# Dense attention with the scores turned over: keys on the partitions, 512 queries moving

## The reference

```
sc = jnp.einsum('bqkgc,bskc->bkgqs', qblk, k).astype(jnp.float32) * scale
p = jax.nn.softmax(sc, axis=-1)
return jnp.einsum('bkgqs,bskc->bqkgc', p.astype(v.dtype), v)
```

## Time and profile before

| | us |
|---|---|
| median of 3 runs (lowest, highest) | 3892.43 (3886.58, 3893.5) |
| span of the profiled execution, first to last instruction | 3884.4 |
| PE busy in the span | 3578.4 (92%) |
| DVE, ACT, POOL busy | 2522.3 (65%), 1854.0 (48%), 255.5 (7%) |
| first instruction of the dense heads to their last product | 2960.4 to 3364.9 |

### The profile page before, as it was taken

How to read it: one execution, slowest core, us unless ns; L and a number is a source line. 1 busy time by engine, 2 the same in 40 slices (tenths; PEclk the granted TensorE clock), 3 DMA queues, 4 the chain that set the end, 5 groups by cost and what they waited for, 6 DMA issues and landing times. The chain is left out here.

```text
span 3884.4 us, 57831 instructions
## 1 busy us (share of the span) xinstructions
PE 3578.4 (92%) x23078; PEld 2954.4 (76%) x23078; DVE 2522.3 (65%) x3931; ACT 1854.0 (48%) x2531; POOL 255.5 (7%) x178
## 2 busy tenths in 40 slices
PE   7999999999999999999999995999888999976996
PEld 5778888777777888877997784777787877765774
DVE  4477673498767667666325645778665766547776
ACT  4224432287334444443215742677436766533775
POOL 0000000000000000000000000233000000002342
PEclk9999999999999999999999997999899999998998
DMA  5011225532513337752413232899623130135998
GB/s 208 28 50 60 87 71 189 187 121 85 182 60 139 149 141 287 261 207 89 145 45 131 62 141 104 329 365 368 200 52 117 37 131 29 48 133 207 366 366 283
DMA packets 229433, 607.63 MB, mean 156 GB/s; under 512 B 30456, under 2 KB 130600, under 8 KB 211136
## 3 DMA queue, kind: packets, MB, share of 16 engines
q1 hardware_dynamic: 212896, 546.91, 38.4%
q0 software_dynamic: 13168, 55.16, 5.0%
q10 hardware_dynamic: 3120, 2.10, 0.2%
HBM read 483.38 MB, written 120.73 MB: 156 GB/s over the span
## 5 line engine op out<-in xcount | busy, mean ns | idle before, releaser
L4459 DVE TENSOR_TENSOR ring_r<-ring,oN_r 128x4096 fp32r<-128x4096 f32 x48 | 212.5, 4427 | 64.5 <-ACT oN_r L4365 64.5
L4459 DVE TENSOR_TENSOR ring_r<-ring,hT_r 128x4096 fp32r<-128x4096 f32 x48 | 212.3, 4424 | 62.1 <-ACT hT_r L4365 62.1
L4365 ACT ACTIVATE hT_r<-ring 128x4096 fp32r<-128x4096 f32 x48 | 174.0, 3630 | 73.1 <-DMA ring<-in_w_all 72.9
L4365 ACT ACTIVATE oN_r<-ring 128x4096 fp32r<-128x4096 f32 x48 | 174.1, 3630 | 68.0 <-DMA ring<-in_w_all 67.2
L171 PE MATMUL scans_G<-ring_r 128*128 128x512 f32 x512 | 204.6, 400 | 0.0
L1433 DVE CUSTOM_DVE_ANT_0 oN<-heads_scores,heads_table 128x1024 f32<-128x1024 f32 x128 | 156.1, 1220 | 42.5 <-issue 42.5
L173 PE MATMUL scans_G<-ring_r 128*128 128x512 f32 x448 | 175.1, 391 | 0.0
L172 PE MATMUL scans_G<-hT_r,ring_r 128*128 128x512 f32 x448 | 175.0, 391 | 0.0
L4237 POOL TENSOR_TENSOR moe_taker<-moe_zero 128x1 f32<-128x1 f32 x64 | 136.5, 2133 | 433.7 <-ACT moe_y L4444 394.0
L1388 ACT ACTIVATE oN<-oN,heads_nm 128x1024 f32<-128x1024 f32 x128 | 146.7, 1146 | 23.4 <-DVE heads_nm L1433 20.2
L172 PE MATMUL mlp_ps<-mlp_room_r,ring_r 128*128 128x512 f32 x384 | 150.4, 392 | 0.0
(11 more groups left out here) (805 smaller groups left out, 10523.0 us busy)
## 6 DMA issues: line engine op xcount, KB each, us to landing
ring<-in_w_all SPq DMA_DIRECT2D x110, 2048.0 KB, 19.1
hidden_operands<-mlp_room SPq DMA_DIRECT2D x56, 512.0 KB, 2.6
ring<-in_w_mlp SPq DMA_DIRECT2D x38, 512.0 KB, 5.5
ring<-in_w_mlp SPq DMA_DIRECT2D x8, 2048.0 KB, 8.1
ring<-in_w_all SPq DMA_DIRECT2D x12, 1024.0 KB, 6.4
branch_gates<-scans_stg SPq DMA_DIRECT2D x48, 256.0 KB, 2.0
merge_raw<-branch_gates SPq DMA_DIRECT2D x16, 768.0 KB, 5.1
ring<-hidden_operands SPq DMA_DIRECT2D x22, 512.0 KB, 3.5
```

The lines of the kernel that those rows point to most:

```text
L4365: act.activation(w_high[n % RING], buf[:, (first + n) % RING, :], ACT.Copy).then_inc(w_cast, 1)
L4459: dve.tensor_tensor(buf_r[:, b, :], buf[:, b, :], w_high[n % RING].bitcast(F32), ALU.subtract)\
```

## The change

The scores are computed with the keys on the partitions: a step takes 128 keys and 512 queries of one pair. Eight steps are a *group* (all keys for 512 queries of a pair), 16 groups in all, 128 steps (`T`). The probabilities then come out of the exponential as the product with the values needs them, so the 1024 transposes, their copies and `shift` go. What the row maximum and the row sum gave must come in other ways:

- **Maxima ahead.** `top(s)` takes the old form (128 queries, 512 keys) in one fp32r pass, for the latent heads with a second pair of products of 32 rows for the rotary part. DVE's `reduce` takes the maxima of it. These run nine steps (`LEAD`) ahead of the scores. At the end of a group PE transposes the maxima (`turn_tops`), and DVE's `shifts` spreads them with a mask.
- **Shift as rows times ones.** For grouped heads a product of 32 rows (`ones_r` with `shift_r`) puts the shift into the scores' bank before the three passes. For latent heads it rides along with the rotary part: its three passes and the shift lie on 128 partitions and are one product of 128 rows per head.
- **Sums.** GpSimd adds up the probabilities of the first seven steps of a group, six additions of 128x1024; PE's `sums` multiplies that and the eighth by ones. DVE takes the reciprocal of 128x512 and multiplies the output, which ACT has copied from PSUM (`keep`), by it.

The splits of queries and keys are cut into pieces of 512 columns (`split_low`) or 1024 (`cast`). The rotary operands use two slots of the weight ring, so during this stage only the two slots of the output projection are loaded; the first two slots of the experts' weights follow in the next stage.

```diff
-        N = PAIRS * NT
-        sc = lent[:, 0:3 * S].rearrange("p (b s) -> p b s", b=3)
-        pT = lent[:, 3 * S:6 * S].rearrange("p (b k n) -> p b k n", b=3, n=P)
...
+        GROUPS = 2 * PAIRS
+        T, LEAD, NP = GROUPS * PER, 9, 6
+        prob = lent[:, 0:NP * S].rearrange("p (b h s) -> p b h s", b=NP, h=2)
+        spare = [(m["ring"].used + 2 + j) % RING for j in range(2)]
...
+        TOPS, SC = st.ps("top_ps", [P, 2, HALF]), st.ps("scores", [P, 2, 2, HALF])
+        O, X = st.ps("outs", [P, HALF]), st.ps("sums", [P, HALF])
+        LOW_AT = {8: (0, 4), 9: (1, 5), 10: (2, 6), 13: (3,), 14: (7,)}
...
+        @block.gpsimd
...
+            for g in range(GROUPS):
+                if g >= 2:
+                    pool.wait_ge(sum_done, g - 1)
+                acc = part[:, g % 2, :, :]
+                for j in range(1, PER - 1):
+                    t = g * PER + j
+                    pool.wait_ge(exped, t + 1)
...
+                    pool.tensor_tensor(acc, prob[:, (t - 1) % NP, :, :] if j == 1 else acc, prob[:, t % NP, :, :], ALU.add)\
+                        .then_inc(pool_added, 1)
 
         @block.tensor
+            def top(s):
...
+                if s:
+                    pe.wait_ge(reduced, s)
...
+                for hd in range(2):
+                    r = slice(64 * hd, 64 * hd + 64)
+                    ins = pe.matmul(TOPS[:, hd, :], q[r, :], k[r, :], start=True, stop=not mla)
+                if mla:
+                    for hd in range(2):
+                        r = slice(32 * hd, 32 * hd + 32)
+                        ins = pe.matmul(TOPS[:, hd, :], rope_q[r, b, hd, toks], rope_k[r, hd, cols], start=False, stop=True)
+                ins.then_inc(topped, 1)
...
+            def turn_tops(g):
+                pe.wait_ge(combined, g + 1)
...
+                    ins = pe.transpose(X[:, 0:P], tops_own[:], m["ident"][:])
+            def score(t):
...
+                if kt == 0:
+                    pe.wait_ge(shifts_in, g + 1)
+                if t >= 2:
+                    pe.wait_ge(exped, t - 1)
+                keys, queries = slice(kt * P, (kt + 1) * P), slice(g % 2 * HALF, (g % 2 + 1) * HALF)
+                if not mla:
+                    for hd in range(2):
+                        r = slice(64 * hd, 64 * hd + 32)
+                        pe.matmul(SC[:, t % 2, hd, :], ones_r[r, :], shift_r[r, g % 2, :], start=True, stop=False)
...
+                for j, (k_, q_) in enumerate(((kh, qh), (kh, ql), (kl, qh))):
+                    for hd in range(2):
+                        r = slice(64 * hd, 64 * hd + 64)
+                        ins = pe.matmul(SC[:, t % 2, hd, :], k_[r, :], q_[r, :], start=mla and j == 0, stop=not mla and j == 2)
+                if mla:
+                    for hd in range(2):
+                        ins = pe.matmul(SC[:, t % 2, hd, :], rope_k[:, hd, keys], rope_q[:, b, hd, queries], start=False,
+                                        stop=True)
...
+            def values(w):
...
+                pe.wait_ge(exped, w + 1)
...
+                    ins = pe.matmul(O[r, :], v[:, b, kt, r] if latent(p) else v[:, b, kt, 0:64], prob[:, w % NP, hd, :],
+                                    start=kt == 0, stop=kt == PER - 1)
...
+            def sums(g):
+                pe.wait_ge(pool_added, (PER - 2) * (g + 1))
...
+                for n, (from_, at) in enumerate(((part, g % 2), (prob, last))):
+                    for hd in range(2):
+                        ins = pe.matmul(X[64 * hd:64 * hd + 64, :], ones[:], from_[:, at, hd, :], start=n == 0, stop=n == 1)
...
+            for t in range(-LEAD, T + 3):
+                s = t + LEAD
+                if s < T:
+                    top(s)
+                if t % PER == PER - 1 and -1 <= t < T - 1:
+                    turn_tops((t + 1) // PER)
+                if 0 <= t < T:
+                    score(t)
+                if t >= PER and t % PER == 2:
+                    sums(t // PER - 1)
+                if 1 <= t <= T:
+                    values(t - 1)
 
         @block.scalar
+            def exp(t):
+                act.wait_ge(scored, t + 1)
...
+                act.activation(prob[:, t % NP, :, :], SC[:, t % 2, :, :], ACT.Exp, scale=scale).then_inc(exped, 1)
 
         @block.vector
+            def reduce(s):
+                dve.wait_ge(topped, s + 1)
...
+                dve.tensor_reduce(tops[:, i % 2, i // 2, :], TOPS[:, :, :], AX.X, ALU.max).then_inc(reduced, 1)
...
+            for t in range(-LEAD, T + 5):
+                s = t + LEAD
+                if s < T:
+                    reduce(s)
...
+                if t >= PER and t % PER == 3:
+                    g = t // PER - 1
+                    dve.wait_ge(sum_done, g + 1)
...
+                    dve.reciprocal(inv[:], X[:]).then_inc(inverted, 1)
+                if t >= PER and t % PER == 4:
...
+                    dve.tensor_tensor(m["hT"][:, (p + GROUPED) % PAIRS, g % 2 * HALF:(g % 2 + 1) * HALF], kept[:, g % 2, :],
+                                      inv[:], ALU.mult).then_inc(normed, 1)
...
@@ build_program
-            m["ring"].limit = m["ring"].total
+            m["ring"].limit = BEFORE_MLP + 1 + 2 + 48 + 1 + 2
             heads_stage(nc, m, qk, qk_low, qk_high)
+        m["ring"].limit = m["ring"].total
```

More of the change, by code:

```diff
@@ L1269, in latent, with upto @@
         def latent(p):
             return p >= GROUPED
+        def upto(counts, p):
+            return sum(counts[:p + 1])
         def loaded(p):
             return 16 * sum(LOADS[p % 2:p + 1:2])
[L1277 to L1278 removed]
         block = st.block()
@@ new lines, in values @@
+            def values(w):
+                g, kt = divmod(w, PER)
+                p = g // 2
+                b = p % 2
+                pe.wait_ge(exped, w + 1)
+                if kt == 0 and g:
+                    pe.wait_ge(kept_in, g)
+                if w % (2 * PER) == 0:
+                    pe.wait_ge(v_in[b], 16 * (p // 2 + 1))
+                for hd in range(2):
+                    r = slice(64 * hd, 64 * hd + 64)
+                    ins = pe.matmul(O[r, :], v[:, b, kt, r] if latent(p) else v[:, b, kt, 0:64], prob[:, w % NP, hd, :],
+                                    start=kt == 0, stop=kt == PER - 1)
+                ins.then_inc(pv_done, 1)
@@ new lines, in _ @@
+            act.wait_ge(m["ident_in"], 16)
+            for n, r in enumerate((0, 64, 96)):
+                of = slice(r, r + 32)
+                act.activation(mask[of, :, :], m["ident"][of, r:r + 4].unsqueeze(2).to_broadcast([32, 4, P]), ACT.Copy,
+                               scale=-1.0).then_inc(mask_in, 1)
+            act.activation(mask[32:64, :, :], m["ident"][32:64, 0:4].unsqueeze(2).to_broadcast([32, 4, P]), ACT.Copy,
+                           scale=-1.0).then_inc(mask_in, 1)
+            for t in range(T):
+                exp(t)
+                if t >= PER and t % PER == 0:
+                    keep(t // PER - 1)
+                p, at = t // (2 * PER) + 1, t % (2 * PER) - 3
+                if p < PAIRS and 0 <= at < HIGHS[p]:
+                    cast(p, at)
+                if p == 2 and at in (7, 8):
+                    hd = at - 7
+                    if hd == 0:
+                        act.wait_ge(key_in, 48)
+                    act.activation(rope_k[0:96, hd, :], key_raw[0:96, :], ACT.Copy).then_inc(key_high, 1)
@@ new lines, in reduce, with combine @@
+            def reduce(s):
+                g, i = divmod(s, PER)
+                dve.wait_ge(topped, s + 1)
+                if g >= 1 and i == 0:
+                    dve.wait_ge(combined, g)
+                dve.tensor_reduce(tops[:, i % 2, i // 2, :], TOPS[:, :, :], AX.X, ALU.max).then_inc(reduced, 1)
+            def combine(g):
+                dve.wait_ge(reduced, PER * (g + 1))
+                if g >= 1:
+                    dve.wait_ge(tops_turned, g)
+                else:
+                    dve.wait_ge(blank, 2)
+                a, b = (tops[:, half, :, :].rearrange("p k h -> p h k") for half in range(2))
+                if latent(g // 2):
+                    out = tops_one[:, :, 96:100]
+                else:
+                    out = tops_own[:, :].rearrange("p (h n) -> p h n", h=2)[:, :, 0:4]
+                dve.tensor_tensor(out, a, b, ALU.max).then_inc(combined, 1)
```

315 lines of the change are left out of this document (153 added, 162 removed).

## The result

The changed kernel takes 3970.79 us (median of four runs, 3963.32 to 3974.84) against 3890.91 for the kernel before in the same runs: 1.0203 times, with a 95% interval of 1.019 to 1.0217. It is 80 us slower; the forecast was 65 us slower, 3957 us. The profiled span grew by 77.2 us, from 3884.4 to 3961.6, and the dense heads by 78.0, from 404.5 to 482.5 (first maxima product to the end of the last normalised output). So the whole difference lies in this stage. I cut it on PE's timeline where the first grouped step, the first latent step and the work behind the last step begin; the forecast's column is made of the prediction's own terms.

A forecast was written before the change was run, and what follows sets the result against it. PE's list bounds the dense heads: 21 + 427 + 2.5 - 7.7 + 17 + 8 = 468 us against 404.5, +65 with the weights; span 3949, median 8.0 above it, so 3957 us, range 3900 to 4005.

The forecast's parts named there:

- Changes of shape at 0.20 us: PE's dense-head steps: each array-shape change costs 0.20 us, four in a 2.75 us grouped step, five in a 3.41 us latent one.
- The rival in which they are free: PE's dense-head steps: array-shape changes cost nothing, steps take 2.0 and 2.46 us, time 3870 us; chance 0.09.
- Nine steps ahead: Start of the dense heads: only maxima run, product and reduction taking turns in one PSUM buffer, 21 us.
- latent steps: Latent half on PE: 3.41 us a step, 29.4 a group; 232.3 us with stalls 4.8 and last nine -7.7.
- the forecast stall of 0.6 us a group: Latent groups: PE's maxima product waits for DVE's reduction queued behind the reciprocal, 7.4 against 6.8 us.
- the one stall I expect: DVE's 3.9 us reciprocal delays the next reduction and PE: 1.5 us a grouped group, 0.6 a latent, 17 us in all.
- the prediction's other estimate, 4.2: DVE's reciprocal by the skill's repeat count of 8: 4.2 us instead of 3.9, making the sum 5 us higher.
- GpSimd's additions: Six a group at 2.8 us each, hidden beneath PE; rival that GpSimd becomes the bound, from 4.2 us each, chance 0.08.
- The first steps at the low level: First steps after the maxima-only start: PE, nearly idle before, runs at its lower clock level, costing 2.5 us.
- the 427 us: PE's list for the dense heads: eight grouped groups of 24.0 us and eight latent of 29.4, against 390 before.
- the three slower cases: Whole kernel: the forecast itself, chance 0.66; a cheap 0.6 us reciprocal, 3937 us, 0.17; GpSimd as the bound, 0.08.
- The end and the weights: After the last step 8 us for exponential, values, sums, reciprocal and waits; experts' first slots loading a stage later, +1.4 us.

The follow-up runs named there:

- doing two steps together: Changed kernel with 64-row shift, reciprocal in PSUM, three-buffer first maxima, PE work paired by two steps, quartered reciprocal, moved splits, earlier casts: 3882.65 us, 0.9982 times the kernel before.
- the short additions: Changed kernel with GpSimd's additions cut from 128x1024 to 128x2, most of the sums left out: 3947.68 us, stage 465.3 against 482.5.
- the run with one input from PSUM: Changed kernel with the reciprocal in place in PSUM, feeding the product, and the largest of two maxima as a one-input reduction: 3962.93 us, stage 476.4 against 482.5.
- the run with busy products: Kernel with steps paired on PE (3882.65 us), plus three idle products behind each of the first nine maxima: 3884.82 us, stage 2.8 us longer.

## Why the prediction was right, and where a size was off

- *Changes of shape at 0.20 us.* Right, and the main term: 2.76 and 3.44 us a step, and 0.195 a change where two were taken away. The rival in which they are free fell with it.
- *Nine steps ahead, latent steps.* 19.0 for 21, 231.1 for 232.3 us. In the latent half the forecast stall of 0.6 us a group did not come, with a reciprocal of 3.35 us for 3.9; in its place PE waited three times 1 us for ACT's cast of rotary operands (L1463), which I had not priced, and a step was 0.01 to 0.03 longer. That this half came out to 1.2 us is therefore luck in part.
- *The reciprocal, "the one stall I expect".* This is the term that was mis-sized: 12 us of stalls in the grouped half, where 225.3 - 198.8 = 26.5 came from DVE. In a plain group the sum came out by luck: the step of the reciprocal is 0.65 us longer than an undisturbed one and the next 0.9, 1.55 for the 1.5 forecast. But the reciprocal was cheaper (3.35 us; the prediction's other estimate, 4.2, was further off than the 3.9 taken), and the second half came from the product held behind GpSimd. Where rotary keys were split or their constant rows written in the same steps, single waits reached 1.6 and 4.1 us, and the lower clock lost 9.7 more, for which the forecast had nothing.
- *GpSimd's additions.* 2.40 us (ninety-six, busy 230 us) for the 2.8 taken, hidden from PE as forecast. I priced them as a bound of their own and not as something that holds DVE; no rival was made of that.
  The Trainium skill (GPSIMD Engine Reference, "8. Key points") says that GpSimd shares its SBUF interface with VectorE and contends with instructions in a 2-port mode or with two SBUF inputs. The runs agree for two SBUF inputs, and give what that section leaves open: DVE waits for the whole rest of the addition (2.62 us for 0.69).
- *The first steps at the low level.* 2.5 us forecast; the second and third step took 4.76 and 4.93 us instead of 2.76, together 4.2 us more. With the first (2.90 without values, for 1.75) and the fourth (3.06) it is 5.6. Nine grouped steps took 2.99, since the maxima ahead of them are latent and have their rotary pair: 2 us that I left out.
- *Sums that do not come out.* One group's sums (1.72 us) and one step's values (1.0) are counted twice, in the 427 us and again in the end: the grouped part holds 7 sums and 63 values, not 8 and 64. These 2.7 us hide as much of what was left out. The chances of the three slower cases add to 0.91, where "slower" has 0.88. The rows of the latent block give 0.09 + 0.10 for a change of shape, not 0.09 + 0.11; 0.195 was measured. The 4.2 us for the reciprocal are eight passes of 0.52 us; the 1.04 named beside them are for 1024 columns, twice as many.
- *The end and the weights.* The output projection takes 85.3 us from its first half tile to its last, as before; the 1.4 us did not come. The end was 0.9 shorter than its term, 0.55 of it the reciprocal.

In sum -2.0 + 18.8 - 1.2 - 0.9 = +14.7 us on the forecast's 468.

## What to carry to other kernels

Count the changes of array shape in a PE list before counting its products: with work cut into small steps, four or five changes at 0.2 us are 0.8 of 2.76 or 1.0 of 3.44 us, and doing two steps together, with the other edits of that run, brought the time back. When GpSimd gets work, list the DVE instructions that read two SBUF tensors and stand in its shadow; an operand in PSUM, or a start outside GpSimd's instructions, takes them out. And two delays on an engine with slack must be tried together and apart: here each alone cost 9.2 or 7.1 us, and both 26.5.

## What the runs showed of the hardware

- A DVE instruction with two SBUF inputs that starts during a GpSimd addition waits for its end, even one of 8 columns (1.92 us for 0.17). One with an input, or its only one, in PSUM does not (0.67 and 1.2 us). With a single SBUF input it depends on the instruction: the constant rows (TENSOR_SCALAR, 32x512, L1550) took 0.42 to 2.55 us, and 0.42 on the mean with the short additions, but the reduction of the maxima (TENSOR_REDUCE, 128x16, in the run with one input from PSUM) took its 0.17 within an addition too.
- It works the other way round as well: the additions that took 2.46 to 2.81 us instead of 2.34 to 2.39 all started while a DVE instruction with two SBUF inputs ran.
- A change of the array's shape between these products cost 0.18 to 0.20 us: 32 to 64 rows and back (2.76 to 2.37 us a step), and 64 rows, 32 rows, full height and 64 columns in a latent pair (6.88 to 6.10).
- DVE's reciprocal takes 3.35 us at 128x512, 0.95 at 128x128 and 0.16 at 128x2: 6.2 to 6.3 ns for each further column.
- PE's lower level came in the grouped part after waits of 1.0 to 4.1 us, but not after every one: four waits of 0.6 to 1.45 us from 3025 to 3035 us were not followed by it. At the stage's start it stayed through 18 us with PE busy for 17.8 of them (the run with busy products).
